# First loads in halves, third slab's sums, output product's tail and GpSimd token rows in a two-block layer kernel

## What is computed

```python
h = layer_norm(ALPHA * x + 0.5 * swiglu(x, ffn1_w_gu, ffn1_w_down), ln_g[0], ln_b[0])
...
merged = jnp.sum(gates * jnp.einsum('bsnc,ncd->bsnd', branches, w_branch), axis=2)
h = layer_norm(ALPHA * h + merged @ w_out, ln_g[1], ln_b[1])
return layer_norm(ALPHA * h + 0.5 * swiglu(h, ffn2_w_gu, ffn2_w_down), ln_g[2], ln_b[2])
```

## Time and profile before

| | |
|---|---|
| median of 3 runs | 3222.66 us (3221.55 to 3223.17) |
| the profiled execution's own time | 3223.21 us |
| its span | 3221.4 us |
| TensorE (matmuls) busy | 2989.7 us, 93% of the span |
| VectorE busy | 2074.9 us, 64% |
| ScalarE busy | 641.3 us, 20% |
| GpSimd busy | 620.7 us, 19% |
| the first block, where the change is | from 0 to about 1570 us of the span |

### The profile page before, as it was taken

One profiled execution on the slowest core, in us unless ns is written; L12 is line 12 of the kernel. 1 busy time (PEld: TensorE's weight loads), 2 busy tenths in 40 slices (PEclk: granted clock), 3 DMA queues, 4 the chain that ended last, 5 costly groups with the idle time before them and its releaser, 6 DMA issues.

```text
span 3221.4 us, 36265 instructions
## 1 busy us (share of the span) xinstructions
PE 2989.7 (93%) x13572; PEld 2007.5 (62%) x13572; DVE 2074.9 (64%) x4762; ACT 641.3 (20%) x1596; POOL 620.7 (19%) x558
## 2 busy tenths in 40 slices
PE   8999999999999999999998888888989988888877
PEld 8958997895986898797685333333448543333322
DVE  7744532776764533476475877777757487777775
ACT  1113121111102223021252111111125321111110
POOL 0010000101001000100012444334421144444442
PEclk9999999999999999999999999999999999999999
DMA  6443323454453323456237999999983599999998
GB/s 232 173 161 131 105 92 131 170 184 157 174 182 143 130 79 111 143 198 242 104 111 274 422 421 418 418 409 417 420 346 125 217 416 421 421 418 414 411 421 349
DMA packets 114943, 830.46 MB, mean 258 GB/s; under 512 B 12880, under 2 KB 13136, under 8 KB 14160
## 3 DMA queue, kind: packets, MB, share of 16 engines
q0 software_dynamic: 73728, 536.90, 40.3%
q1 hardware_dynamic: 39456, 281.29, 24.2%
q10 hardware_dynamic: 1584, 9.95, 0.8%
HBM read 827.05 MB, written 1.05 MB: 257 GB/s over the span
## 4 chain that ended last, share of the span: by engine, by line
PE 63%; DMA 23%; DVE 8%; issue 5%; ACT 1%; POOL 1%; POOLq 0%; DVEq 0%; SPq 0%; ACTq 0%
DMA arena<-table_uv,idx 23%; PE bank L473 11%; PE bank L535 8%; PE bank L2458 8%; PE bank L379 6%; PE bank L711 5%; PE bank L460 4%; PE bank L947 3%; PE bank L2145 3%; PE bank L2330 2%; PE bank L406 2%; DVE arena L3084 1%; DVE arena L2821 1%; PE bank L609 1%; DVE diag L3092 1%
## 5 line engine op out<-in xcount | busy, mean ns | idle before, releaser
L2458 PE MATMUL bank<-arena,diag 128*128 128x512 f32 x2048 | 1014.6, 621 | 191.9 <-DVE diag L3092 184.9
L2458 PEld LDWEIGHTS bank<-arena,diag 128*128 128x128 f32 x2048 | 359.5, 191 | 722.8 <-DVE diag L3092 460.7
L3084 DVE CUSTOM_DVE_ANT_0 arena<-arena 128x1024 f32<-128x1024 f32 x512 | 625.5, 1222 | 256.2 <-DMA arena<-table_uv,idx 253.2
L3169 POOL DMA_INDIRECT arena<-table_uv,idx x512 | 543.5, 1061 | 927.5 <-PE bank L2458 710.9
L2698 ACT ACTIVATE dots<-dots 128x1 f32<-128x1 f32 x512 | 103.9, 203 | 1089.4 <-DVE dots L3084 1089.0
L1824 POOL TENSOR_TENSOR x_tok<-arena,ktail 128x1024 f32<-128x1024 f32 (+1 forms) x12 | 27.8, 2313 | 1513.7 <-ACT arena L976 1513.7
L460 PE MATMUL bank<-x,ring 128*128 128x128 f32 x1408 | 173.8, 278 | 12.9 <-DMA ring<-stream 12.9
L3092 DVE TENSOR_SCALAR diag<-cst,dots,soft 128x128 f32<-128x128 f32 x512 | 175.9, 344 | 0.0
L460 PEld LDWEIGHTS bank<-x,ring 128*128 128x128 f32 x1408 | 166.7, 194 | 14.1 <-issue 9.4
L711 PE MATMUL bank<-x,ring 128*128 128x256 f32 x768 | 173.1, 379 | 0.0
L379 PE MATMUL bank<-x,ring 128*128 128x256 f32 x768 | 170.5, 384 | 0.0
(11 more groups left out here) (651 smaller groups left out, 4321.6 us busy)
## 6 DMA issues: line engine op xcount, KB each, us to landing
ring<-stream SPq DMA_DIRECT2D x258, 1024.0 KB, 4.8
arena<-table_uv,idx POOLq DMA_INDIRECT x512, 13.0
ktail<-ln_rows ACTq DMA_DIRECT2D x6, 1024.0 KB, 4.8
arena<-mem_rows SPq DMA_DIRECT2D x2, 1024.0 KB, 10.6
arena<-stream SPq DMA_DIRECT2D x2, 1024.0 KB, 7.3
sq<-keys ACTq DMA_DIRECT2D x2, 1024.0 KB, 4.7
cst<-consts SPq DMA_DIRECT2D x1, 1547.0 KB, 8.0
cst<-consts SPq DMA_DIRECT2D x1, 1089.0 KB, 14.8
```

The lines of the kernel that those rows point to most:

```text
L2458: last = mm(bank[4 + 2 * tt + half][:, :], diag[:, n % DIAGS, :], row_slot(n)[:, D + 512 * half:D + 512 * half + 512], start=(h == 0 and k ...
L3084: v.tensor_tensor_reduce(u, u, tok[:, tt, :], 1.0, 0.0, ALU.mult, ALU.add, dots[:, tt, k:k + 1]).then_inc(u_used.sem, 1)
L3169: g.indirect_dma_start(out=row_slot(n), out_offset=None, in_=peer_uv, in_offset=bass.IndirectOffsetOnAxis(ap=idx[:, h % 2, tt, k:k + 1], a ...
```

## The change

Five edits:

- At the start, SP loads the first half of `x`, the first half of slab 0, the second half of `x`, and then the second half of slab 0, in four transfers of 512 KB in place of two of 1 MB. TensorE's first four matmuls wait for the first two of these, and the next four for the third.
- In the first feed-forward part, VectorE forms the sums of slab 2 ahead of the adding up of slab 0, not behind it.
- In the second tile's share of the output product, the first two of the last three slabs are finished whole (4 matmuls each) ahead of the transposes, and then the last slab's two halves follow (2 and 2). `acc_done`, which lets VectorE add the first half of tile 1's residual, moves from ahead of the transposes to behind the last slab's first half.
- In the feed-forward parts other than the first and the last, `first_tile(2)` moves from ahead of `both_tiles(0)` to behind `both_tiles(1)`.
- GpSimd's rows behind the second and third norm (but not the very last) wait: those of tile 0 until slab 1 of the next feed-forward part has been added up (`gu_summed` of 2), those of tile 1 until slab 5 has (`gu_summed` of 6).

```diff
+ROWS_BEHIND = (2, 6)
...
-            sp.dma_start(x[:, :, :], x_in).then_inc(x_loaded, 16)
-            for n in range(RING):
+            low, high = slice(0, KC // 2), slice(KC // 2, KC)
+            sp.dma_start(x[:, low, :], x_in[:, low, :]).then_inc(x_loaded, 16)
+            first = ring[:, 0].rearrange("p b n -> p (b n)")
+            sp.dma_start(first[:, 0:D], stream[0, :, 0:D]).then_inc(first_half_loaded, 16)
+            sp.dma_start(x[:, high, :], x_in[:, high, :]).then_inc(x_loaded, 16)
+            sp.wait_ge(slab_done.sem, 1)
+            sp.dma_start(first[:, D:2 * D], stream[0, :, D:2 * D]).then_inc(slab_loaded[0].sem, 16)
+            for n in range(1, RING):
                 fetch(n)
...
+                for w in tail[:-1]:
+                    for half in range(2):
+                        for r in range(2):
+                            last = part(w, r, 1, half)
+                    last.then_inc(slab_done.sem, 1)
+                to_channels(l, n, 0, y)
                 for half in range(2):
                     for r in range(2):
-                        last = part(tail[0], r, 1, half)
+                        last = part(tail[-1], r, 1, half)
+                    if half == 0:
+                        last.then_inc(acc_done.sem, 1)
                 last.then_inc(slab_done.sem, 1)
-                for w in tail[1:]:
-                    for r in range(2):
-                        last = part(w, r, 1, 0)
-                last.then_inc(acc_done.sem, 1)
-                to_channels(l, n, 0, y)
-                for w in tail[1:]:
-                    for r in range(2):
-                        last = part(w, r, 1, 1)
-                    last.then_inc(slab_done.sem, 1)
...
-                first_tile(2)
+                ahead = BANKS if first or last_stage(l, f) else BANKS - 1
+                if ahead == BANKS:
+                    first_tile(2)
                 if not first:
                     x_waits(l, n, 1)
                 for j in range(GU_SLABS):
-                    if j >= BANKS:
+                    if j >= ahead:
                         first_tile(j)
                     both_tiles(j)
...
                 weight_sums(l, f, at, 1)
+                if l == 0 and f == 0:
+                    weight_sums(l, f, at, 2)
...
-                    weight_sums(l, f, at, j + 2)
+                    if l > 0 or f > 0 or j > 0:
+                        weight_sums(l, f, at, j + 2)
...
+                        if n == 1:
+                            pool.wait_ge(gu_summed.sem, gu_summed.at(l, FC + ROWS_BEHIND[tt]))
+                        elif n == 2 and not final:
+                            pool.wait_ge(gu_summed.sem, gu_summed.at(l + 1, ROWS_BEHIND[tt]))
```

More of the change, by code:

```diff
@@ L266, in first_block @@
         x_loaded = sem("x_loaded")
+        first_half_loaded = sem("first_half_loaded")
         mem_loaded = sem("mem_loaded")
@@ L454, in first_tile @@
                 def first_tile(j):
-                    w, out = slab(l, at + j), bank[W_X[j % BANKS]]
+                    if first and j == 0:
+                        pe.wait_ge(first_half_loaded, 16)
+                        w = ring[:, 0]
+                    else:
+                        w = slab(l, at + j)
+                    out = bank[W_X[j % BANKS]]
                     free(j)
                     for at_k, lo in ((0, 0), (KC // 2, P)):
+                        if first and j == 0 and lo > 0:
+                            pe.wait_ge(x_loaded, 32)
                         for k in range(KC // 2):
@@ L1306, in weight_sums @@
                 dve.wait_ge(loaded.sem, loaded.at(l, 16 * (slab // RING + 1)))
+                if l == 0 and f == 0 and i == 0:
+                    dve.wait_ge(first_half_loaded, 16)
                 if i >= GU_SLABS + 3:
@@ L1325, in x_sums @@
                 if l == 0 and f == 0:
-                    dve.wait_ge(x_loaded, 16)
+                    dve.wait_ge(x_loaded, 32)
                 else:
```

## The result

The changed kernel takes 3231.37 us (median of 7 runs, 3229.45 to 3236.15), the kernel before 3222.66 us beside it (7 runs, 3220.62 to 3223.17). The ratio is 1.0029, with a 95% interval of 1.0020 to 1.0038: the change makes the kernel slower, by some 9 us. The span of the profiled execution grew from 3221.4 to 3229.5 us.

The account below looks back on a forecast made before the run. TensorE, busy 93% of the span, was taken as the bound, so only its waits count. Gains 1.7+3.0 = 4.7 and losses 1.8+0.85+6.25 = 8.9 gave 4.2 us slower than 3222.66: 3226.9, rounded to 3227, range 3219 to 3230.5.

Parts of the forecast that it names:

- the start: First loads in halves: TensorE starts 2.5 us earlier but then waits for slabs 1 and 2; 0.35 us gained.
- the rows: GpSimd's row pairs collide with VectorE's sums in three feed-forward parts; TensorE waits 5 x 0.75 + 2.5, 6.25 us lost.
- Of the 2.5 us 0.35 remain: At the kernel's start, the third MB of loads sets the time, so 0.35 us of the 2.5 earlier start is won.
- nothing behind it: At the start, halved loads change the order within the first 2 MB only; slabs 1 and 2 land at 11.3 and 13.8.
- The third slab's sums: First feed-forward part: forming slab 2's sums early removes TensorE's wait of 1.34 us at that slab.
- Seams 1 and 2: Entering the two middle feed-forward parts: `first_tile(2)` was hidden beside VectorE's chain, so moving it loses 1.8 and 0.85 us.
- Seam 3: Ahead of the last feed-forward part: slab 1 is issued 2.5 us earlier and `both_tiles(0)` starts earlier; 3.0 us gained.
- GpSimd is quiet now: Ahead of the last feed-forward part: VectorE's sums of slab 0 run without GpSimd beside them, within the 3.0 us gain.
- The rival of a fall behind the new waits: TensorE's clock falls in new idle time: one fall 3228.6 us, chance 0.25; two 3230.3, two or more 0.15.

Follow-up runs that it names:

- after_no_rows: The changed kernel without the wait of GpSimd's rows for slabs 1 and 5; 3228.25 us, ratio 1.0014.
- ft2_alone: The kernel before with only `first_tile(2)` moved behind `both_tiles(1)` in the two middle feed-forward parts; 3226.80 us, ratio 1.0014.
- tail_alone: The kernel before with only the output product's end done slab by slab; 3224.18 us, ratio 1.0004.
- rows_alone: The kernel before with only the wait of GpSimd's rows for slabs 1 and 5; 3233.89 us, ratio 1.0039.
- after_spread: The changed kernel with GpSimd's four row operations one by one behind slabs 5, 7, 9 and 11, not in two pairs; 3222.52 us, ratio 0.9995.
- after_ft2_ahead: The changed kernel with `first_tile(2)` ahead of `both_tiles(0)` in every feed-forward part; 3235.95 us, ratio 1.0039.
- halves_alone: The kernel before with only the first loads in halves; 3224.71 us, ratio 1.0007.

## Why the prediction was wrong

The direction was right and most of the mechanisms were those forecast, but 4.2 us of loss were forecast and 8.7 measured: 3226.9, with a range up to 3230.5, against 3231.37. The steps of the prediction come to 6.4 when each is taken as the trace has it. Two terms make this difference: the start, whose mechanism was wrong and which lost 0.8 where 0.35 were to be won (1.1), and the rows, whose mechanism was right and whose size was too small (1.5). With every step put right the sum is 3229.1, still inside the range; the last 2.3 us have no cause that the runs show. Step by step:

- **The start: the step that failed in its mechanism.** "Of the 2.5 us 0.35 remain" took the first sixteen passes at the slow rate and all behind the wait for slab 1 at the fast one, with slabs 1 and 2 at 11.3 and 13.8. The runs showed a loss: `both_tiles(0)` starts at 15.3 to 16.1 in the eight profiles with whole loads and at 16.1 to 18.1 in the five with halves and nothing in the wait. Two things were missed. The first is the loads: "nothing behind it" was wrong. In the six profiles with halves slab 1 came at 11.7 to 11.8, in seven with whole loads at 10.6 to 10.9 and once, in the profile that I predicted from, at 11.28; that one run hid half of this. By this alone the forecast 15.7 becomes 16.1 (`after_no_rows`, all passes behind the wait fast), so that nothing is won. That it comes of four issues in place of two is likely but was not tried by itself. The second is the slow passes: in four of the five profiles there were more of them behind the wait, 0.7 us' worth in the changed kernel. What decides whether they come stays open; it is not the wait alone, as `after_no_rows` shows, and the kernels with whole loads have from 14 to 24 slow passes at their start too, without a wait.
- **The third slab's sums.** 1.34 forecast, 1.5 measured, no wait in its place.
- **Seams 1 and 2.** 1.8 and 0.85 forecast. The chain of VectorE set `both_tiles(1)` in both, as said; `first_tile(2)` cost its 1.79 in each, and seam 2 gave 0.88 back. `ft2_alone` agrees with 3.6 in the time and 3.4 in the trace.
- **Seam 3.** 3.0 forecast, 3.25 measured, by the steps given: 1.13 on `x` of tile 0, none on the load. That it depends on the rows being away was implied in "GpSimd is quiet now" and is shown by `tail_alone`.
- **The rows: the term that was too small.** 6.25 forecast, 7.8 in the trace. The waits are 0.83 and 2.60 (0.75 and 2.5 forecast), but TensorE's steps are later by 0.8 to 1.1 and 2.75: about 0.2 more for each wait, which the idle column does not hold, since a matmul's modelled end reaches past the start of the next and the first eight passes behind a wait are slower (1.13 in place of 1.06). `rows_alone` gives 10.6 net of what it wins in seam 3, where slab 3 has no `first_tile(2)` to help, and `after_spread` 8.9 for the pairs in the change.
- **The clock.** The rival of a fall behind the new waits did not happen in the profile of the changed kernel, though its wait at slab 3 of the last part was 2.60; it happened behind one of the three such waits (2.3 to 2.6) in `rows_alone`, behind one of three in `after_ft2_ahead`, and behind both of the waits of 4.24 (`tail_alone`, `after_no_rows`). So it depends on more than the wait's length, and it is a cost in some executions.
- **The rest: not explained.** 1.7 us of the profiled difference arose in the second block, late in it: the same matmul is 5.1 later near 2600 us and 7.3 near 2700. In the other profiles the second block's share scattered between 1.4 us less and 1.8 more than in the kernel before, with no relation to the edits that I can name, and the places of the clock's falls differ from run to run. I take it for scatter, which was argued and not shown; no run here settles whether the changed kernel has a part of it for good.

## What to carry to other kernels

When work is moved off a critical seam, ask what slack the place has that it is moved to, against the whole length of what is moved in one piece: two operations in one place made TensorE wait 0.8 to 2.6 us each time, the same two at different slabs made it wait at one operation of twelve, 0.4 us. Judge a reordering by the chain that ends last behind it, not by the wait that one sees: `first_tile(2)` stood behind a wait for a load, and moving it away from there only took it out of a shadow. And an engine that starts earlier but has to wait for its second load has won nothing by it: look for the load that sets the time, and read its landing from more than one profile, since it moved by 0.7 us from run to run here.

## What the runs showed of the hardware that I had not expected

- GpSimd's 128x1024 operation stopped VectorE's sums with two SBUF inputs until it was through (2.84 in place of 0.69 us) and left additions with one input in PSUM at their time (0.42).
- The number of slow passes (0.21 us) at the start differs from run to run: 14 to 24 in the kernels with whole loads. With a wait for slab 1 behind the first sixteen, thirteen to twenty-five more followed in four of five profiles (in `halves_alone` with a granted clock of 0.50) and hardly any in the fifth.
- The lower level came in some executions behind a wait of 2.6 us and in others not.
- A fall of the clock near 250 us of the first block came once in seven of the fourteen profiles, for twice as long in three, and not at all in four; each moves the time by 1.7 us, as much as several of the edits studied here. In the kernel before TensorE ran 32 passes of eight columns ahead of it (3.63 us) without idle time.
- Splitting 2 MB of first loads into four transfers made what comes behind them 0.8 to 1.2 us later (0.4 against the one late profile).
